# A decoder block with window attention and a mixture of experts: two copies of attention moved ahead of exponentials, and two final squares and roots moved into ScalarE's step loop

## The reference

```
h = rmsnorm(x)
q, k, v, xr, yr, ga, gl = split(h @ w_in)
y_attn = sliding_window_attention(rope(q), rope(k), v, sinks) @ w_attn_o   # 8 blocks of 128 queries, 256 keys
y_lru  = (rg_lru(conv(xr)) * gelu(yr)) @ w_lru_o
x = x + (sigmoid(ga) * y_attn + sigmoid(gl) * y_lru) @ w_out
h = rmsnorm(x)
x = x + moe(h)            # top 4 of 32 experts: gate_up 1024 x 2048, down 1024 x 1024
return rmsnorm(x)         # the final norm: square, mean, root, scale
```

## Time and profile before

| what | value |
|---|---|
| median of 3 runs | 2066.96 us (2064.79 to 2067.16) |
| the profiled execution, its own time | 2066.78 us |
| its span, first instruction to last | 2065.1 us |
| PE busy | 1976.0 us, 96% |
| DVE busy | 1572.8 us, 76% |
| ACT busy | 1284.4 us, 62% |
| POOL busy | 300.3 us, 15% |
| share of PE in the chain that ended last | 89% |
| attention | about 130 to 275 us from the start |
| the step loop | about 655 to 2034 us |

### The profile page before, as it was taken

One profiled execution on the slowest core, in us unless ns is written; L12 is line 12 of the kernel. 1 busy time (PEld: TensorE's weight loads), 2 busy tenths in 40 slices (PEclk: granted clock), 3 DMA queues, 4 the chain that ended last, 5 costly groups with the idle time before them and its releaser, 6 DMA issues.

```text
span 2065.1 us, 37029 instructions
## 1 busy us (share of the span) xinstructions
PE 1976.0 (96%) x11800; PEld 1533.5 (74%) x11801; DVE 1572.8 (76%) x2038; ACT 1284.4 (62%) x1772; POOL 300.3 (15%) x340
## 2 busy tenths in 40 slices
PE   7999899999996999999999999999999999999993
PEld 6777678888685777777777778877777877777783
DVE  5788756566657879788777779977878988976896
ACT  5555455454544667667666658765667767755775
POOL 3100000000135211102222111211111101221110
PEclk9999999999997999999999999999999999999997
DMA  5030111011545978989877799979889979878994
GB/s 182 21 102 1 42 41 41 21 41 41 162 178 155 331 255 307 358 289 370 291 273 275 265 337 380 339 264 338 294 287 374 378 284 370 314 268 280 377 373 192
DMA packets 256272, 489.98 MB, mean 237 GB/s; under 512 B 20203, under 2 KB 38471, under 8 KB 256128
## 3 DMA queue, kind: packets, MB, share of 16 engines
q1 hardware_dynamic: 233824, 439.56, 58.8%
q0 software_dynamic: 21360, 49.81, 9.1%
q10 hardware_dynamic: 1040, 0.00, 0.0%
HBM read 461.66 MB, written 32.18 MB: 239 GB/s over the span
## 4 chain that ended last, share of the span: by engine, by line
PE 89%; DVE 5%; issue 2%; ACT 2%; DMA 1%; POOL 0%; POOLq 0%; ACTq 0%; SPq 0%; DVEq 0%
PE psum L828 17%; PE psum L829 17%; PE psum L832 17%; PE psum L841 8%; PE psum L507 3%; PE psum L509 3%; PE psum L640 3%; PE psum L508 3%; PE psum L814 3%; PE psum L642 3%; PE psum L644 3%; PE psum L788 1%; PE psum L858 1%; PE psum L761 1%; PE psum L762 1%
## 5 line engine op out<-in xcount | busy, mean ns | idle before, releaser
L1890 DVE TENSOR_TENSOR w_lo<-ring,w_hi 128x1024 fp32r<-128x1024 f32 x768 | 910.2, 1221 | 101.3 <-ACT w_hi L1185 89.4
L1185 ACT ACTIVATE w_hi<-ring 128x1024 fp32r<-128x1024 f32 x768 | 790.0, 1058 | 132.5 <-PE psum L832 128.9
L828 PE MATMUL psum<-w_hi,rows_hi 128*128 128x512 f32 x1024 | 426.3, 416 | 0.0
L829 PE MATMUL psum<-w_hi,rows_lo 128*128 128x512 f32 x1024 | 400.5, 391 | 0.0
L832 PE MATMUL psum<-w_lo,rows_hi 128*128 128x512 f32 x1024 | 316.5, 390 | 0.0
L832 PEld LDWEIGHTS psum<-w_lo,rows_hi 128*128 128x128 f32 x1024 | 192.8, 188 | 41.3
L829 PEld LDWEIGHTS psum<-w_hi,rows_lo 128*128 128x128 f32 x1024 | 193.5, 189 | 38.3
L828 PEld LDWEIGHTS psum<-w_hi,rows_hi 128*128 128x128 f32 x1024 | 194.0, 189 | 37.4
L828 PE MATMUL psum<-w_hi,act_hi 128*128 128x512 f32 x512 | 215.6, 421 | 0.0
L829 PE MATMUL psum<-w_hi,act_lo 128*128 128x512 f32 x512 | 199.8, 390 | 0.0
L841 PE MATMUL psum<-ring,region_m 128*32 128x256 f32 x3072 | 171.9, 379 | 0.0
(11 more groups left out here) (359 smaller groups left out, 3042.6 us busy)
## 6 DMA issues: line engine op xcount, KB each, us to landing
ring<-in_w_gate_up_dram SPq DMA_DIRECT2D x128, 2048.0 KB
ring<-in_w_down_dram SPq DMA_DIRECT2D x64, 2048.0 KB, 12.6
ring<-in_w_in_dram SPq DMA_DIRECT2D x16, 512.0 KB, 5.2
region_m<-in_x_dram SPq DMA_DIRECT2D x8, 512.0 KB, 11.6
ring<-in_w_in_dram SPq DMA_DIRECT2D x2, 2048.0 KB, 15.8
ring<-in_w_out_dram SPq DMA_DIRECT2D x2, 2048.0 KB, 7.7
region_a<-in_x_dram POOLq DMA_DIRECT2D x8, 512.0 KB, 5.3
acc_rows<-region_a POOLq DMA_DIRECT2D x8, 512.0 KB, 3.8
```

Source lines behind the costliest of these rows:

```text
L828: mm(bank(i), hi[:, ks], wh, start=False, stop=False)
L829: mm(bank(i), lo[:, ks], wh, start=False, stop=False)
L1185: act.activation(w_hi[:, n % NBUF, :], place[i][:, k0 * HALF:(k0 + 2) * HALF], ACT.Copy).then_inc(hi_done, 1)
L1890: v.tensor_tensor(out=w_lo[:, n % NBUF, :], in0=place[i][:, k0 * HALF:(k0 + 2) * HALF], in1=w_hi[:, n % NBUF, :].bitcast(f32), op=ALU.subt ...
```

## The change

In attention, `qkT_out(1)` goes ahead of both groups of exponentials of block 0, `qkT_out(7)` ahead of the second group of block 6, and PE turns the first half of block 0's probabilities (`turn_prob(0, 0)`) in the middle of pass 2's k, v projection, right ahead of the second half. In the step loop, `final_square(0)` and `final_square(1)` stand at the end of each of the two unrolled steps, under the condition that no step follows; the eight others stay behind the loop.

```diff
@@ PE
                 project_q(s, range(4, 6))
-                if s >= 2:
+                if s >= 3:
                     turn_prob(s - 2, 0)
                 project_q(s, range(6, KD))
                 scores(s - 1)
                 if s >= 2:
                     project_kv(s, range(0, 4))
+                    if s == 2:
+                        turn_prob(0, 0)
                     turn_prob(s - 2, 1)
@@ ScalarE, attention
             qkT_out(0)
+            qkT_out(1)
             exps(0, 0)
             exps(0, 1)
             for s in range(2, NT + 1):
-                qkT_out(s - 1)
+                if 3 <= s < NT:
+                    qkT_out(s - 1)
                 pT_out(s - 2, 0)
...
                 exps(s - 1, 0)
                 oT_out(s - 2)
+                if s == NT - 1:
+                    qkT_out(NT - 1)
                 if s == NT:
                     gate_high(2)
                 exps(s - 1, 1)
@@ ScalarE, step loop
+                                with act.If(more < 1):
+                                    final_square(0)
+                                    final_square(1)
                                 act.nop()
                     act.nop()
 
-            for n in range(len(FINAL)):
+            for n in range(2, len(FINAL)):
                 final_square(n)
```

## The result

| | before | after |
|---|---|---|
| median | 2067.06 us of 6 runs (2064.79 to 2069.23) | 2078.39 us of 6 runs (2077.52 to 2081.38) |
| profiled execution, time and span | 2066.78, 2065.1 us | 2077.81, 2076.1 us |

The ratio is 1.0056, 95% interval 1.0045 to 1.0066: 11.6 us slower. Split by stages, from the trace: the last product of the step loop's first piece starts at 671.1 us instead of 676.2 (5.1 earlier); from there to the last product's end the loop takes 1371.0 us instead of 1357.5 (13.6 longer, unrounded); from that end to the end of the span it is 34.0 us instead of 31.4 (2.6 longer). But for rounding that makes 11.0, the difference of the spans.

The account below looks back on a forecast made before the run. PE was taken to bound the step loop, doing nothing but work there, while attention stopped it twice. From 2066.8 us, minus 6.5 (attention), plus 14.4 (loop) and 2.8 (end), gave 2077.5 us, range 2069 to 2086.

Parts of the forecast that it names:

- The first stop: Attention, PE's 4.04 us wait ahead of the first turning of probabilities: gain 0.6 us, the rest going into other PE waits.
- The second stop: Attention, PE's 3.98 us wait ahead of the last scores: shrinks to 1.4 us, clock stays up, gain 6.3 us.
- The 0.4 taken off for a falling clock: Attention: deduction for the chance that gaps near 252, 254 or ahead of 175.5 lower PE's clock, 1.7 us a time.
- The load ahead of `high(4)`: Step loop, ScalarE: a 1.28 us table load in every step, made good by `high(8)` through the buffers, cost nothing.
- The load ahead of `sigmoid(0)`: Step loop: makes VectorE 1.41 us late and `actT_low(0)` 0.8 us late, paid in 16 steps without a tail.
- The handing over of `up_part(0)`: Step loop: 1.41 us late against 1.41 in hand, so about 0.1 us in each of 16 steps with a tail.
- "Nothing in hand": Step loop, piece 16: PE loads the bias 0.42 us after `actT_low(0)` ends, so without a tail lateness there is paid.
- The end: Behind the loop: way out behind the second root and loads around the third square, 2.8 us lost.
- Rival 1: Step loop: the loads cost PE nothing, or merge; 2063.1 us, faster if attention gives 8; chance 0.12.
- Rival 2: Step loop: a switch holds ScalarE twice as long, 2.8 us for 1.41; about 2124 us; chance 0.05.
- Rival 3: Attention: the clock falls again at the remaining gaps, gain 2 us instead of 6.5; 2082 us; chance 0.10.

Follow-up runs that it names:

- experiment 5: Kernel before with the attention part for the first stop alone (`qkT_out(1)` ahead, first turning moved), block 7 as before: ratio 0.9997 (0.9987 to 1.0006).
- experiment 3: Changed kernel plus a one-column Sigmoid ahead of each step's `high(4)`, leaving one table load a step, at its start: ratio 0.9991 of before.
- experiment 4: Changed kernel with VectorE's `actT_low(0)` placed ahead of `low(16)` instead of behind it, loads unchanged: ratio 0.9986 of before.
- experiment 12: Kernel before with the attention part and `actT_low(0)` ahead of `low(16)`, roots behind the loop, no small Exp: ratio 0.9958, median 2058.86 us.
- experiment 1: Kernel before with the attention part of the change alone, final squares and roots behind the loop: ratio 0.9971, median 2059.98 us.
- experiment 6: Kernel before with the second stop's part alone, block 7's copies directly behind `oT_out(5)`: ratio 0.9974 (0.9964 to 0.9983).
- experiment 7: Kernel before with the attention part and a one-column Exp between `qkT_out(0)` and `qkT_out(1)`: ratio 0.9968 (0.9955 to 0.9980).
- experiment 11: Kernel before with the attention part, a one-column Exp between `qkT_out(0)` and `qkT_out(1)`, and `actT_low(0)` ahead of `low(16)`: ratio 0.9954, median 2057.05 us.
- experiment 9: Kernel before with a one-column Exp ahead of each step's first sigmoid, so two loads stand there: 2125.43 us in one run.
- experiment 10: Kernel before with VectorE's `actT_low(0)` placed ahead of `low(16)`, no loads in the loop: ratio 0.9981 (0.9972 to 0.9990).
- experiment 8: Kernel before with only the first two final squares inside the step loop, their two roots behind it: ratio 1.0001 (0.9991 to 1.0010).

## Why the prediction was right

- **The first stop**, 0.6 us: that most of the 4 us would go into other waits of PE is shown, at 163 and 175 in the trace and by experiment 5's interval. So are the inner numbers: exponentials from 155.28 (1.7 later than the earlier trace rows), rotation at 162.85 where 162.9 was forecast. The 0.6 itself isn't confirmed (experiment 5).
- **The second stop**, 6.3: 5.4 (3.5 to 7.4) alone, and PE 7 us ahead in all behind the attention. The 0.4 taken off for a falling clock was fair, though the profile after doesn't show it: there the clock stayed at 1.00 from 250 us on, but in experiments 3, 4 and 12, with the same attention, it fell to 0.50 right behind the gaps near 252 and 254. From the last but one scores to the turning of the last block it is 26.8 us in the changed kernel and in experiments 1, 6, 7 and 11, and 28.2 to 28.4 in those three: 1.4 to 1.6 a time where 1.7 was put, in three of eight. The kernels without this part of the change take 30.6 to 33.2, the profiled one of before 33.1, so that the 7 us of the profiled pair are the favourable end. 6.5 forecast for the attention, 6.0 (3.7 to 8.5) measured.
- **The load ahead of `high(4)`**, nothing: shown by experiment 3, where a load at the step's start stands alone. Together with the second load it wasn't quite nothing: in two steps behind a tail, as the 37.22 us one above, 0.33 us of it reached the sigmoid, and the step was 0.36 longer than its neighbour.
- **The load ahead of `sigmoid(0)`**, 0.8 in steps without a tail: 0.80 in the step shown, 13.3 us over 16 waits. Experiments 4 and 9 show the way it takes: moved ahead, the product takes the loss away; a longer delay grows it by as much. The trace of before bore the number because the two small idles of VectorE and the 1.41 in hand at `up_part(0)` could be read off it.
- **The handing over of `up_part(0)`**, 0.1 in steps with a tail: wrong, they are 48.64 as before. That is 1.6 us of the sum's 14.4. The loop grew by 13.6, more than 16 x 0.8 = 12.8, as those two steps grew by 1.2 and most others without a tail by a little over 0.80.
- **"Nothing in hand"** at piece 16 was half right: PE had less than nothing, 0.17 of loss already (experiment 10). The sum didn't need it, as it went by differences.
- **The end**, 2.8: 2.6, by the two loads around the third square and the way out behind the second root. That is read from the trace; no run has the end alone.
- **How near the total came** is in part luck: 2077.5 was forecast and the profiled execution took 2077.8, but its attention gave 7.0 us and 2 of them were lost again ahead of the loop, in a wait that the sum doesn't have.
- **Rival 1** (the loads cost nothing, or merge) failed at both: two loads a step, and 13.3 us of waits. By the rule of the Trainium skill ("ScalarE activation tables: per-element evaluation and per-set limits", "Table sets in the compiler and the runtime") the copy and the sigmoid would share one; the trace shows a load at each, and experiment 3 had to ask for the merged one by hand. **Rival 2** (twice the length) failed: the activation behind a load starts 0.01 us after its row ends, and the sigmoid is 1.41 late, not 2.8. The page "ScalarE: Activation LUTs" of the Trainium skill, "What ACT_TABLE_LOAD costs", adds about 1380 ns of drain to its 1283; the trace agrees with the 1283 and shows no drain, here in 32 loads squeezed between busy neighbours. Experiment 9 is what a delay of that size costs: its loop grew by 60.8 us where the rival put 58. That its time of 2125 us is near the rival's 2124 is chance, since that kernel has neither the gain in attention nor the loss at the end. **Rival 3** (attention gives 2 us) failed by experiment 1, whose interval begins at 3.7; the falling clock that it built on did come, behind the stop at 163 in the changed kernel at no cost, and near 252 in three of the runs at 1.4 to 1.6 us.

What stays open: why the granted clock falls behind a gap in one execution and not in another with the same code up to there, and why the wait for the first gathered rows changes by 3 us.

## What to carry to other kernels

A root inside the step loop, under a condition that is true once, made the built program reload sets in every pass, also ahead of a copy; a square at the same place did not (experiment 8). Look at the built order, not at the source. Whether a load costs is a matter of its place: 32 at the start of the steps cost nothing, 32 ahead of an activation that feeds a tight handover cost 13 us, and one dummy activation of the right function at an idle place moves them. Where an engine "waits for nothing" ahead of a handover, try the producer one instruction earlier: that alone was worth 3.9 us (2.1 to 5.8) in the kernel before. And where a stop of some us shows a low clock in one profile, look at a second one before counting on the difference.

## What was not expected of the hardware

- PE's clock behind equal gaps: 1.9 us of idle at about 175 us, then a granted clock of 1.00 in one kernel and 0.57 and 0.69 in two others. What is won in front of such a place can be lost right behind it. The same with equal code: behind the 2.62 to 2.63 us of idle at 163, the clock of the window from 164 to 166 was 1.00 in experiments 1 and 3, and 0.58, 0.50 and 0.50 in the changed kernel and experiments 4 and 12.
- ScalarE's way out of the loop takes 2.4 us with nothing busy (2.38 behind the last output, 2.43 behind the second root); behind the squares alone 1.61 of it show (experiment 8).
- The wait for the first indirect gather took 4.33, 5.45 and 2.29 us in three kernels with the same code there.
